# Moving a page compression by part of a unit against the delta-rule core that hides it

## The chip, the cores and the metric

The program runs on one core of one Trainium2 chip. The metric is the device time of one execution in microseconds: 1716.98 us is the median of three (1714.06 to 1723.23). TensorE (PE) multiplies, VectorE (DVE), ScalarE (ACT) and GpSimd (POOL) work on tiles, SyncE (SP) issues most transfers; a q behind an engine's name is its sequencer.

## What is computed

One inference step of a two-layer trunk: a gated DeltaNet layer and a sparse-attention layer (NSA), each followed by a gated feed-forward layer with a short convolution. There are 256 new tokens of one prompt and 8 x 8 tokens of running sequences, which have 1024 past positions in pages. Two parts matter here. The delta rule of 16 heads, evaluated in chunks:

```python
a_mat = where(stri, (kb @ k.T) * decay, 0) + eye          # unit lower triangular, inverted by levels
u, w = solve(a_mat, v * beta), solve(a_mat, kb * exp(gcum))
v_new = u - w @ s;  o = q_dec @ s + qk @ v_new;  s = s * g_tot + k_dec.T @ v_new
```

And the compression of the past pages, which needs nothing of the first layer and so is done beside it:

```python
first  = einsum('bnsgd,sdh->bngh', sub + pe[0], w1[0])    # sub: blocks of 16 past rows
second = einsum('bnsgd,sdh->bngh', sub + pe[1], w1[1])
hid = silu(first[:, :-1] + second[:, 1:]);  out = hid @ w2   # once for keys, once for values
```

## The kernel before, in words

The core stage works through eight **units** i = 0 to 7, in a loop of four run twice. A unit does the delta rule of one pair of heads (h = 0, 1) and the compression for two sequences: units 0 to 3 compress keys (v = 0), units 4 to 7 values (v = 1). No tile is doubled for the loop; each engine has one hand-written order, and semaphores counted by step name hold them together (`Steps.count(name, i)`).

*The delta rule on TensorE* (`pe_core_pair`, L1180): Gram products (L1191, L1198), turned keys (`ktok`, L1195), row broadcasts (L1206), then the inverse of the triangular matrix. Levels 1 to 4 are the **small products** (L1217, L1221: eight groups, `cp1`, `cx1` to `cp4`, `cx4`, 48 or 32 matmuls of 32 x 32), each waiting for VectorE (`dve_core`, L1394: masks, subtraction, transpose; the final spreading to full tiles X and Y is L1468). Levels 5 and 6 are full products (L1234, L1242, L1250), then come turned values (L1259), the state products (L1270, `ks`), v0, s1, ks1, v1, s2, o (L1277 to L1306) and the sample state update (L1316, `snew`).

*The compression* has 8 row groups m per unit. `turn_rows` (L1085): four transposes of raw page rows into the one bank 7. `copy_turned_rows` (L1136) on ScalarE: four copies out of the bank (L1143), which free it, and one rounding copy (L1146). `low_rows` (L1539, L1543) on POOL: the rest that rounding lost. `turned` has two buffers, by m % 2. `hidden_part` (L1097): 12 products for each m (L1107), cut in four **pieces** n = 4 m to 4 m + 3 of three products; the third product of piece 4 m + 2 is the first that reads the low part. `fill(lo, hi)` puts pieces lo to hi - 1 between the steps of the delta rule, where TensorE would wait. After piece 31 ScalarE applies silu (`hidden_silu`, L1151, with a table load), TensorE makes the **final product** (`compressed_rows`, L1118: L1125, L1132) into bank 7, and ScalarE stages it (`stage_compressed`, L1153).

The order of the turns before: turn 0 after the Gram products (L1200), 1 after the broadcasts, pieces 0 to 3, turn 2, pieces 4 to 7; pieces 8 to 15 between the small products, with turns 3 (at 9) and 4 (at 13); turn 5, 16, 17; level 5 with 18, 19, turn 6; level 6 with 20; 21 before `ks`; 22 and 23 after v0; s1, **turn 7** (L1286), ks1, 24 and 25, v1, 26 and 27, s2, o, 28 to 31, snew, final product.

*SP* (`sp_compress`, L1012) loads the raw rows in two halves x = 0, 1, one transfer of 64 KB for each of 16 pages, each with a page number read from SBUF (L1026). Half 0 holds the rows of turns 0 to 3, half 1 those of turns 4 to 7, and each is loaded for the next unit after turn 3 or 7 of this one. In order: half 0 of the next unit, half 1 of the next unit, then `store_pair` (L1028): after `snew` of each head the sample states (L1032) and the prompt state (L1033), then, after the staging copy, the compressed rows (L1036, L1038). Between units 3 and 4 it differs: half 0, eight loads of value weights (L1046, after each piece group of unit 3), `store_pair(3)`, and only then half 1.

*POOL* (`pool_core_pair`, L1537), in order: low parts 0 and 1, masks (`kmask`, L1552, after the key and query copies), a wait until the four state stores of the previous unit have landed (L1555), two state loads into the tiles so freed (L1557), low parts 2 to 6, two scalings of the state (L1562, after `ks`), low part 7, two spreads (L1567, after v0), for which snew waits. In unit 4 it also splits the value weights ahead of each low part (`split_w1`, L1529: L1533, L1535).

```python
            pool.wait_ge(state_out, STATES * i + 16)          # L1555
            for h in range(2):
                pool.dma_start(hd[h]["S0"], ...).then_inc(state_in, 16)
            for m in range(2, 7):
                low_rows(m)
```

Of the kernel before, what the change touches and what calls it, by code (L numbers as in the profile page):

```python
# [29 lines left out]
P = 128  # L30
# [198 lines left out]
def build(nc, ins, outs, where, base_cols):  # L229
    ctx = ExitStack()  # L230
    with ctx:
# [720 lines left out]
        for h in hd:  # L952
# [14 lines left out]
            pe=steps("core_pe", ["gram0", "ktok", "gram"] + both(["rows"])  # L967
# [7 lines left out]
            act=steps("core_act", both(["v"]) + ["ktok"] + both(["egc", "dec", "kdec", "r"]) + both(["qs"]) + both(["o"]) + ["k", "q"], lag=True),  # L975
            pool=steps("core_pool", ["lo0", "lo1", "kmask"] + [f"lo{m}" for m in range(2, 7)] + ["s0g0", "s0g1", "lo7", "spread0", "spread1"], lag=True))
# [31 lines left out]
            pe=steps("cmp_pe", ["t0", "t1", "u0"] + [x for m in range(2, 8) for x in (f"t{m}", f"u{m - 1}")] + ["h0", "u7", "o"], lag=True),  # L1008
            act=steps("cmp_act", [f"{x}{m}" for m in range(8) for x in "cr"] + ["h0", "h1", "s"], loop=True))
        H_BANK, T_BANK = (5, 6), 7  # L1010

        def sp_compress(sp):  # L1012
# [15 lines left out]
            def store_pair(g, v):  # L1028
# [5 lines left out]
                sp.wait_ge(C["act"].sem, C["act"].count("s", i))  # L1034
# [29 lines left out]
            sp.wait_ge(C["pe"].sem, C["pe"].count("o", UNITS_CMP - 1))  # L1064
# [20 lines left out]
        def turn_rows(pe, u, m):  # L1085
            if m % 4 == 0:
                pe.wait_ge(raw_in[m // 4], 256 * (u + 1))
            pe.wait_ge(C["act"].sem, C["act"].count(f"c{m - 1}", u) if m else C["act"].all_before(u))
# [3 lines left out]
            last.then_inc(C["pe"].sem, C["pe"].step(f"t{m}"))  # L1092
# [4 lines left out]
        def hidden_part(pe, u, v, n):  # L1097
            m, piece = n // 4, n % 4
            if piece == 0:
                pe.wait_ge(w1_split, 8 * v + m + 1)  # L1100
                pe.wait_ge(C["act"].sem, C["act"].count(f"r{m}", u))
            for t, half, part in HIGH_FIRST[3 * piece:3 * piece + 3]:
                if part == "low_rows" and t == 0 and half == 0:
                    pe.wait_ge(S5["pool"].sem, S5["pool"].count(f"lo{m}", u))
# [4 lines left out]
                if part == "low_rows" and half == 1:  # L1109
                    if t == 1:  # L1110
                        last.then_inc(C["pe"].sem, C["pe"].step(f"u{m}"))
# [6 lines left out]
        def compressed_rows(pe, u, v):  # L1118
            pe.wait_ge(C["act"].sem, C["act"].count("h1", u))
# [14 lines left out]
            last.then_inc(C["pe"].sem, C["pe"].step("o"))  # L1134

        def copy_turned_rows(act, u, m):  # L1136
            act.wait_ge(C["pe"].sem, C["pe"].count(f"t{m}", u))
            act.wait_ge(C["pe"].sem, C["pe"].count(f"u{m - 2}", u) if m >= 2 else C["pe"].count(f"u{m + 6}", u - 1))
# [5 lines left out]
            last.then_inc(C["act"].sem, C["act"].step(f"c{m}"))  # L1144
            act.wait_ge(C["act"].sem, C["act"].count(f"c{m}", u))
            act.copy(turned_high[m % TURNED], turned[m % TURNED]).then_inc(C["act"].sem, C["act"].step(f"r{m}"))  # L1146

        def hidden_silu(act, u, v, t):
            act.wait_ge(C["pe"].sem, C["pe"].count("h0" if t == 0 else "u7", u))
            act.wait_ge(C["pe"].sem, C["pe"].count("o", u - 1))  # L1150
            act.activation(cmp_hid[t].rearrange("p (x n) -> p x n", x=8), psum[:, H_BANK[t], 0:4 * NC2].rearrange("p (n x) -> p x n", x=8), ACT.Silu, bias=pe_bias[:, 2 * v + t:2 * v + t + 1]).then_inc(C["act"].sem, C["act"].step(f"h{t}"))  # L1151

        def stage_compressed(act, g, u, v):  # L1153
            act.wait_ge(C["pe"].sem, C["pe"].count("o", u))
# [7 lines left out]
            ins_.then_inc(C["act"].sem, C["act"].step("s"))  # L1162
# [7 lines left out]
        def pe_core(pe):  # L1170
            pe.sem_inc(S5["pe"].sem, S5["pe"].first)
            pe.sem_inc(C["pe"].sem, C["pe"].first)
# [3 lines left out]
            for v in range(2):  # L1176
                with pe.Fori(0, 4) as g:
                    pe_core_pair(pe, g + 4 * v, v)

        def pe_core_pair(pe, i, v):  # L1180
# [3 lines left out]
            def fill(lo, hi):  # L1184
                for n in range(lo, hi):
                    hidden_part(pe, i, v, n)
# [5 lines left out]
            last.then_inc(pe_steps.sem, pe_steps.step("gram0"))  # L1192
            pe.wait_ge(dve_steps.sem, dve_steps.all_before(i))
            for u in range(3):
                last = pe.transpose(psum[:, B_BANK[1], u * P:(u + 1) * P], kS[:, u * P:(u + 1) * P], ident)  # L1195
            last.then_inc(pe_steps.sem, pe_steps.step("ktok"))
            for rhs, cols in ((kS, G_COLS), (qS, Q_COLS)):
                last = pe.matmul(psum[:, A_BANK[0], cols], kS[:, TP:TP + P], rhs[:, TP:T], start=True, stop=True)  # L1198
            last.then_inc(pe_steps.sem, pe_steps.step("gram"))
            turn_rows(pe, i, 0)  # L1200
            pe.wait_ge(dve_steps.sem, dve_steps.all_before(i))
            for q, banks in ((0, A_BANK), (1, B_BANK)):
                for h in range(2):
                    if q == 1 and h == 1:
                        pe.wait_ge(act_steps.sem, act_steps.count("ktok", i))
                    last = pe.matmul(psum[:, banks[h], 0:T], row_ones[h], row_src[h][:, q, :], start=True, stop=True)  # L1206
                    if q == 1:
                        last.then_inc(pe_steps.sem, pe_steps.step(f"rows{h}"))
# [1765 lines left out]
```

## Time and profile before

| | |
|---|---|
| three executions | 1716.98, 1714.06, 1723.23 us |
| span of the profiled execution | 1715.5 us |
| mean granted clock of TensorE | 0.943 of full |
| busy: PE, DVE, ACT, POOL | 90%, 56%, 47%, 17% |
| core stage, first Gram product to last final product | 254.8 to 712.1 us |
| units 0 to 7 | 57.1, 55.0, 54.9, 54.7, 62.8, 55.4, 55.3, 62.1 us |

The profiled execution is one more execution: its span runs from the first to the last instruction, and lies 1.5 us under the median of the executions, which also have what lies around the instructions. Times in rows are from the span's start; a number in brackets is the idle time of the engine ahead of the group, with what ended it.

### The profile page before, as it was taken

The numbers are of one execution on the slowest core, as the hardware profiler recorded it, in microseconds if no ns is written. First come the engines' busy times: TensorE is split into PE (matmuls) and PEld (weight loads), VectorE is DVE, ScalarE is ACT, GpSimd is POOL, SyncE is SP. The second block draws the span as 40 slices with busy tenths as digits, with TensorE's granted clock in tenths as the row PEclk, the third lists the DMA queues.
The fourth block names the chain that finished last, engine by engine and source line by source line (L and its number), as shares of the span: only waits on it lengthen the run. The fifth ranks groups of instructions, "written<-read, shape, count | busy, mean of one in ns | idle before, by whom it ended". The sixth has DMA issues, their size and how long they took to land.

```text
span 1715.5 us, 38118 instructions
## 1 busy us (share of the span) xinstructions
PE 1539.0 (90%) x13678; PEld 1348.7 (79%) x13678; DVE 952.5 (56%) x1749; ACT 800.6 (47%) x1579; POOL 300.1 (17%) x492
## 2 busy tenths in 40 slices
PE   6999979999988998899999999966777778999897
PEld 6999847777757776579999999954555558999897
DVE  5775245554655454464777644434655556777732
ACT  5675325665555555443444533224444535444521
POOL 1331033433454332200000001031112100000000
PEclk9999969999999998979999999997898987999999
DMA  7444232322432232425555658444534414555650
GB/s 179 147 144 157 102 117 58 95 76 59 125 100 71 66 89 75 112 66 147 148 147 147 174 134 227 128 151 143 169 98 161 132 50 123 147 147 147 164 135 31
DMA packets 285294, 209.56 MB, mean 122 GB/s; under 512 B 29231, under 2 KB 277071, under 8 KB 284768
## 3 DMA queue, kind: packets, MB, share of 16 engines
q1 hardware_dynamic: 275926, 176.32, 36.9%
q0 software_dynamic: 9248, 31.80, 6.0%
q8 instruction: 45, 0.74, 0.2%
q10 hardware_dynamic: 42, 0.44, 0.1%
q14 instruction: 33, 0.27, 0.1%
HBM read 185.67 MB, written 22.85 MB: 122 GB/s over the span
## 4 chain that ended last, share of the span: by engine, by line
PE 74%; DVE 8%; ACT 7%; issue 5%; DMA 2%; SPq 1%; POOL 1%; POOLq 1%; DVEq 0%; ACTq 0%
PE psum L621 15%; PE psum L622 15%; PE psum L623 15%; PE psum L1107 7%; ACT sbuf_resident L2429 2%; PE psum L1221 1%; PE psum L2226 1%; PE psum L1091 1%; PE psum L2381 1%; DMA sbuf_resident<-in_nsa_w_in_dram 1%; PE psum L1610 1%; PE psum L915 1%; PE psum L1270 1%; PE psum L1234 1%; PE psum L1250 1%
## 5 line engine op out<-in xcount | busy, mean ns | idle before, releaser
L621 PE MATMUL psum<-h_rounded,weights_low 128*128 128x320 f32 x1248 | 392.0, 314 | 1.9 <-DVE weights_low L597 1.9
L623 PE MATMUL psum<-h_rounded,weights_high 128*128 128x320 f32 x1248 | 387.0, 310 | 0.0
L622 PE MATMUL psum<-weighted_x_low,weights_high 128*128 128x320 f32 x864 | 267.2, 309 | 0.0
L621 PEld LDWEIGHTS psum<-h_rounded,weights_low 128*128 128x128 f32 x1248 | 235.2, 188 | 5.1 <-DVE weights_low L597 2.1
L597 DVE TENSOR_TENSOR weights_low<-sbuf_resident,weights_high 128x2048 fp32r<-128x2048 f32 x90 | 205.7, 2288 | 55.1 <-ACT weights_high L582 55.1
L623 PEld LDWEIGHTS psum<-h_rounded,weights_high 128*128 128x128 f32 x1248 | 235.1, 188 | 0.0
L582 ACT CAST weights_high<-sbuf_resident 128x2048 fp32r<-128x2048 f32 x90 | 170.1, 1893 | 95.1 <-PE psum L623 64.8
L622 PEld LDWEIGHTS psum<-weighted_x_low,weights_high 128*128 128x128 f32 x864 | 165.9, 192 | 0.2
L1143 ACT COPY sbuf_resident<-psum 64x256 f32<-64x256 f32 x256 | 108.5, 424 | 91.3 <-PE psum L1091 88.8
L696 DVE SCALAR_TENSOR_TENSOR sbuf_stages<-sbuf_stages,sbuf_resident 128x344 f32<-128x344 f32 (+1 forms) x184 | 105.6, 574 | 55.5 <-ACT sbuf_stages L678 51.7
L1543 POOL TENSOR_TENSOR turned_low<-sbuf_resident,turned_high 128x512 fp32r<-128x512 f32 x64 | 76.8, 1200 | 265.3 <-ACT turned_high L1146 265.2
L678 ACT ACTIVATE sbuf_stages<-sbuf_stages,sbuf_resident 128x336 f32<-128x336 f32 (+1 forms) x76 | 44.1, 581 | 165.0 <-DVE sbuf_stages L1774 164.0
L622 PE MATMUL psum<-weights_low,weights_high 128*128 128x320 f32 x384 | 118.8, 309 | 0.0
L686 POOL COPY sbuf_stages<-sbuf_stages 128x2 f32<-128x2 f32 (+1 forms) x76 | 30.8, 405 | 494.5 <-DVE sbuf_stages L1774 417.8
L621 PE MATMUL psum<-hidden_high,weights_low 128*128 128x320 f32 x352 | 110.9, 315 | 6.3 <-ACT sbuf_resident L1731 5.4
L1107 PE MATMUL psum<-turned_high,w_low 128*128 128x504 f32 x256 | 114.6, 448 | 1.9 <-POOL w_low L1535 1.9
L622 PE MATMUL psum<-hidden_low,weights_high_wide 128*128 128x320 f32 x352 | 110.0, 313 | 0.0
L623 PE MATMUL psum<-hidden_high,weights_high_wide 128*128 128x320 f32 x352 | 109.8, 312 | 0.0
L1107 PE MATMUL psum<-turned_high,w_high 128*128 128x504 f32 x256 | 106.6, 416 | 0.0
L1107 PE MATMUL psum<-turned_low,w_high 128*128 128x504 f32 x256 | 75.1, 400 | 2.8 <-POOL turned_low L1543 2.8
L1645 DVE TENSOR_TENSOR sbuf_resident<-sbuf_resident,psum 128x320 f32<-128x320 f32 x24 | 11.7, 487 | 118.1 <-PE psum L623 118.1
L622 PEld LDWEIGHTS psum<-weights_low,weights_high 128*128 128x128 f32 x384 | 73.4, 191 | 0.0
(438 smaller groups left out, 3147.7 us busy)
## 6 DMA issues: line engine op xcount, KB each, us to landing
sbuf_resident<-in_ffn_w_up_dram SPq DMA_DIRECT2D x88, 512.0 KB, 4.9
sbuf_resident<-in_gdn_w_in_dram SPq DMA_DIRECT2D x48, 512.0 KB, 4.7
sbuf_resident<-in_ffn_w_down_dram SPq DMA_DIRECT2D x32, 704.0 KB, 6.3
sbuf_resident<-in_cache_nsa_kv_dram SPq DMA_DIRECT2D x256, 64.0 KB
sbuf_stages<-in_state_gdn_s_dram POOLq DMA_DIRECT2D x16, 512.0 KB, 5.3
out_gdn_s_sample_dram<-sbuf_stages SPq DMA_DIRECT2D x16, 512.0 KB, 3.8
sbuf_resident<-in_gdn_w_out_dram SPq DMA_DIRECT2D x16, 512.0 KB, 5.5
sbuf_stages<-in_cache_nsa_kv_dram POOLq DMA_DIRECT2D x64, 128.0 KB, 3.4
```

The lines of the kernel that those rows point to most:

```text
L582: act.copy(dst[:, 0:kn * P], slot(w)[:, 0:kn * P]).then_inc(hi_done, 1)
L597: eng.tensor_tensor(ring_lo[w % RING][:, 0:kn * P], sl, hi[:, 0:kn * P], ALU.subtract).then_inc(lo_done, 1)
L621: pe.matmul(out, w_lo, x_hi_tile, start=first, stop=False)
L622: pe.matmul(out, w_hi, x_lo_tile, start=False, stop=False)
L623: return pe.matmul(out, w_hi, x_hi_tile, start=False, stop=last)
L678: return act.activation(y[:, 0:n_out], xp[:, 0:n_out], ACT.Copy, scale=tap)
L686: pool.tensor_copy(tail[:, 0:hist], xp[:, TP:TP + hist])
L696: dve.scalar_tensor_tensor(out=y[:, 0:n_out], in0=xp[:, n:n + n_out], scalar=taps(n), in1=y[:, 0:n_out], op0=ALU.mult, op1=ALU.add).then_i ...
L1107: last = pe.matmul(psum[:, H_BANK[t], 0:4 * NC2], weights[:, 8 * half + m, t * P:(t + 1) * P], rows, start=(m == 0 and half == 0 and part ...
L1143: last = act.copy(dst, src)
L1543: pool.tensor_tensor(turned_low[m % TURNED], turned[m % TURNED], turned_high[m % TURNED], ALU.subtract).then_inc(pool_steps.sem, pool_step ...
L2429: return act.activation(s, s, ACT.Exp, bias=mx_p[:, h, x:x + 1], accum_out=sm_p[:, h, x:x + 1])
```

## The change

Each unit's turn 0 and its copy, rounding and low part move to the end of the previous unit; for unit 0 they stand ahead of the loop. The final product and the staging copy move into the next unit, behind pieces 1 to 3 and behind the exponentials `egc`; those of unit 7 stand behind the loop. The first and last unit and unit 4 have bodies of their own, with the counts adjusted. SP's order and the order of its waits stay; its wait for the staging copy is for the moved copy. POOL's order stays but for low part 0, now the last of the previous unit. The core of the diff, as the new order of TensorE:

```diff
+            turn_rows(pe, i, 1)                # after the first Gram products
+            fill(0, 1)
             pe.wait_ge(dve_steps.sem, dve_steps.all_before(i))
-            ktok transposes; late Gram products; turn_rows(pe, i, 0); row broadcasts (h = 1 waits for ktok's copy)
-            turn_rows(pe, i, 1)
-            fill(0, 4)
-            turn_rows(pe, i, 2)
-            fill(4, 8)
+            late Gram products; row broadcasts
+            fill(1, 4)
+            if place != "first":
+                compressed_rows(pe, i - 1, before)
+            pe.wait_ge(dve_steps.sem, dve_steps.count("bts1", i))
+            ktok transposes
+            turn_rows(pe, i, 2, first=place == "first")      # waits for the staging copy of i - 1
+            fill(4, 10)
+            turn_rows(pe, i, 3)
+            fill(10, 12)
+            pe.wait_ge(act_steps.sem, act_steps.count("ktok", i))
             for k in range(1, SMALL):
...
-                    n = 8 + 2 * (k - 1) + (name == "cx")
-                    if n % 4 == 1:
-                        turn_rows(pe, i, 3 + (n - 8) // 4)
+                    n = 12 + 2 * (k - 1) + (name == "cx")
                     fill(n, n + 1)
-            turn_rows(pe, i, 5)
-            fill(16, 18)
+                    if n in (13, 17):
+                        turn_rows(pe, i, 4 if n == 13 else 5)
+            fill(20, 21)
...
-                fill(18 if k == SMALL else 20, 19 if k == SMALL else 21)
+                fill(21 if k == SMALL else 23, 22 if k == SMALL else 24)
...
-                    fill(19, 20)
                     turn_rows(pe, i, 6)
+                    fill(22, 23)
...
-                    fill(21, 22)               # ahead of ks
+                    fill(24, 25)
...
-            fill(22, 24)                       # behind v0; turn 7 stays behind s1
+            fill(25, 27)
...
-            fill(24, 26)                       # behind ks1
+            fill(27, 28)
...
-            fill(26, 28)                       # behind v1
+            if place != "last":
+                turn_rows(pe, i + 1, 0)
+            fill(28, 30)
...
-            fill(28, 32)                       # behind o
+            fill(30, 32)
...
-            compressed_rows(pe, i, v)
```

(Lines such as "late Gram products; row broadcasts" put several statements in words.) Two waits are new: piece 0 waits for the previous unit's second silu, and turn 2 for its staging copy. ScalarE's new order:

```diff
-            v copies; ktok; copy_turned_rows 0; egc; dec; copy_turned_rows 1, 2; kdec; 3, 4, 5; r; qs; 6, 7; o; k, q; silu; stage
+            copy_turned_rows 1; egc; stage of i - 1; dec; ktok; 2; v copies; 3; kdec; 4, 5, 6; r; qs; 7; 0 of i + 1; o; k, q; silu
```

And POOL's:

```diff
+            if split:
+                split_w1(pool, v, 0)
-            low_rows(0)
-            low_rows(1)
+            low_part_of(1)
             kmask; wait for the state stores; state loads; low parts 2 to 6; s0g; low part 7; spreads
+            if not is_last:
+                low_rows(pool, i + 1, 0).then_inc(pool_steps.sem, pool_steps.step("lo0next"))
```

## Rows read from the trace of the kernel before

**Rows 1.** The profile page: busy time by engine, and the chain that ended last.
```profile
PE 1539.0 (90%) x13678; PEld 1348.7 (79%) x13678; DVE 952.5 (56%) x1749; ACT 800.6 (47%) x1579; POOL 300.1 (17%) x492
...
PE 74%; DVE 8%; ACT 7%; issue 5%; DMA 2%; SPq 1%; POOL 1%; POOLq 1%; DVEq 0%; ACTq 0%
```

**Rows 2.** Stretches, units 2 and 4: length; busy PE, PEld, DVE, ACT, POOL; clock, DMA.
```profile
366.90:421.80 54.90, 51.94 (x664) 40.51 (x662) 30.95 (x76) 31.07 (x70) 18.96 (x16) 1.00 0.29 82
...
476.50:539.30 62.80, 54.69 (x680) 42.46 (x678) 31.18 (x76) 31.31 (x70) 32.12 (x30) 0.95 0.30 82
```

**Rows 3.** Timeline of TensorE, unit 2; the last two lines are of units 4, 7.
```profile
371.88 0.66 PE L1091 MATMUL psum<-sbuf_resident 128*128 128x128 f32 x4 [0.82 <-ACT sbuf_resident L1143]
...
376.79 0.66 PE L1091 MATMUL psum<-sbuf_resident 128*128 128x128 f32 x4 [1.28 <-ACT sbuf_resident L1143]
...
478.78 1.34 PE L1206 MATMUL psum<-sbuf_stages,sbuf_resident 16*128 16x320 f32 x8
...
660.44 0.66 PE L1091 MATMUL psum<-sbuf_resident 128*128 128x128 f32 x4 [2.56 <-ACT sbuf_resident L1143]
```

**Rows 4.** Timelines of TensorE, SP and POOL, from turn 7 of unit 1.
```profile
354.49 0.60 PE L1091 MATMUL psum<-sbuf_resident 128*128 128x128 f32 x4
...
378.24 0.62 SPq L1033 DMA_DIRECT2D out_gdn_s_prompt_dram<-sbuf_stages  x1
...
382.30 1.80 POOL L1557 DMA_DIRECT2D sbuf_stages<-in_state_gdn_s_dram  x2 [2.02 <-DMA out_gdn_s_prompt_dram<-sbuf_stages]
384.11 1.29 POOL L1543 TENSOR_TENSOR turned_low<-sbuf_resident,turned_high 128x512 fp32r<-128x512 f32 x1
...
385.78 0.39 PE L1107 MATMUL psum<-turned_low,w_high 128*128 128x504 f32 x1
...
409.32 0.60 PE L1091 MATMUL psum<-sbuf_resident 128*128 128x128 f32 x4
...
410.10 20.20 SPq L1026 DMA_DIRECT2D sbuf_resident<-in_cache_nsa_kv_dram  x16
```

**Rows 5.** Timelines of TensorE and VectorE in unit 2: small products and spreading.
```profile
380.96 0.23 PE L1217 MATMUL psum<-sbuf_resident 128*32 128x8 f32 x2 [0.53 <-DVE sbuf_resident L1439]
...
381.67 0.50 PE L1107 MATMUL psum<-turned_high,w_low 128*128 128x504 f32 x1
...
382.55 0.23 PE L1217 MATMUL psum<-sbuf_resident 128*32 128x8 f32 x2
...
392.41 0.23 PE L1217 MATMUL psum<-sbuf_resident 128*32 128x8 f32 x2
...
393.83 1.92 DVE L1468 TENSOR_TENSOR sbuf_stages<-sbuf_resident 128x256 f32<-128x256 f32 x4
...
395.53 1.05 PE L1234 MATMUL psum<-sbuf_stages 128*128 128x128 f32 x8
```

**Rows 6.** Timelines of ScalarE, POOL and TensorE in unit 2, behind turn 7.
```profile
410.03 1.74 ACT L1143 COPY sbuf_resident<-psum 64x256 f32<-64x256 f32 x4 [1.21 <-PE psum L1091]
...
414.93 2.28 POOL L1567 TENSOR_TENSOR sbuf_stages<-sbuf_stages,sbuf_resident 64x512 f32<-64x512 f32 x2
...
421.75 1.16 PE L1191 MATMUL psum<-sbuf_stages 128*128 128x128 f32 x8
```

**Rows 7.** Unit 7: timelines of POOL and TensorE; a stretch (columns as rows 2).
```profile
671.12 0.89 POOL L1557 DMA_DIRECT2D sbuf_stages<-in_state_gdn_s_dram  x1 [4.41 <-issue]
...
673.35 0.49 PE L1107 MATMUL psum<-turned_low,w_high 128*128 128x504 f32 x1 [2.81 <-POOL turned_low L1543]
...
673.35:685.81 12.46, 12.46 (x216) 8.98 (x217) 4.47 (x14) 3.39 (x8) 2.27 (x2) 0.73 0.10 35
```

**Rows 8.** Timelines of SP and TensorE in unit 4.
```profile
478.78 1.19 SPq L1036 DMA_DIRECT2D compressed_keys<-sbuf_resident  x1
481.51 23.43 SPq L1026 DMA_DIRECT2D sbuf_resident<-in_cache_nsa_kv_dram  x18
...
504.55 1.11 PE L1091 MATMUL psum<-sbuf_resident 128*128 128x128 f32 x4 [2.20 <-DMA sbuf_resident<-in_cache_nsa_kv_dram]
```

More of the change, by code:

```diff
@@ L966, in build @@
         S5 = dict(
-            pe=steps("core_pe", ["gram0", "ktok", "gram"] + both(["rows"])
+            pe=steps("core_pe", ["gram0", "gram"] + both(["rows"]) + ["ktok"]
                      + [f"{x}{k}" for k in range(1, SMALL) for x in ("cp", "cx")]
@@ L1007, in build, with c_count, low_rows_count @@
         C = dict(
-            pe=steps("cmp_pe", ["t0", "t1", "u0"] + [x for m in range(2, 8) for x in (f"t{m}", f"u{m - 1}")] + ["h0", "u7", "o"], lag=True),
-            act=steps("cmp_act", [f"{x}{m}" for m in range(8) for x in "cr"] + ["h0", "h1", "s"], loop=True))
+            pe=steps("cmp_pe", ["t1", "u0", "o_prev", "t2", "u1"] + [x for m in range(3, 8) for x in (f"t{m}", f"u{m - 1}")] + ["t0next", "h0", "u7"], lag=True),
+            act=steps("cmp_act", ["c1", "r1", "s_prev"] + [f"{x}{m}" for m in range(2, 8) for x in "cr"] + ["c0next", "r0next", "h0", "h1"], lag=True))
+        def c_count(eng, name, u):
+            if name in ("t0", "c0", "r0"):
+                if isinstance(u, int) and u == 0:
+                    return C[eng].first - (name == "c0")
+                return C[eng].count(f"{name}next", u - 1)
+            if name in ("o", "s"):
+                if isinstance(u, int) and u == UNITS_CMP - 1:
+                    return C[eng].all_before(UNITS_CMP, 1)
+                return C[eng].count(f"{name}_prev", u + 1)
+            return C[eng].count(name, u)
+        def low_rows_count(m, u):
+            return S5["pool"].count("lo0next", u - 1) if m == 0 else S5["pool"].count(f"lo{m}", u)
         H_BANK, T_BANK = (5, 6), 7
@@ L1171, in pe_core @@
             pe.sem_inc(S5["pe"].sem, S5["pe"].first)
[L1172 removed]
+            pe.sem_inc(C["pe"].sem, C["pe"].first - 1)
             pe.wait_ge(pads, 11)
@@ L1175, in pe_core, with pe_core_pair @@
             pe.wait_ge(bias_act, 2)
[L1176 to L1180, printed above, removed]
+            turn_rows(pe, 0, 0, first=True)
+            pe_core_pair(pe, 0, 0, "first")
+            with pe.Fori(1, 4) as i:
+                pe_core_pair(pe, i, 0)
+            pe_core_pair(pe, 4, 1)
+            with pe.Fori(5, 7) as i:
+                pe_core_pair(pe, i, 1)
+            pe_core_pair(pe, 7, 1, "last")
+            compressed_rows(pe, 7, 1, last_unit=True)
+        def pe_core_pair(pe, i, v, place=None):
+            before = 0 if place != "first" and (v == 0 or isinstance(i, int) and i == 4) else 1
             pe_steps, dve_steps, act_steps, pool_steps = S5["pe"], S5["dve"], S5["act"], S5["pool"]
@@ L1332, in act_core @@
                 take(act, 0, x).then_inc(S5["act"].sem, 1)
-            for v in range(2):
-                with act.Fori(0, 4) as g:
-                    act_core_pair(act, g, g + 4 * v, v)
+            copy_turned_rows(act, 0, 0, first=True)
+            act_core_pair(act, 0, 0, 0, "first")
+            with act.Fori(1, 4) as i:
+                act_core_pair(act, i, i, 0)
+            act_core_pair(act, 4, 4, 1)
+            with act.Fori(5, 7) as i:
+                act_core_pair(act, i - 4, i, 1)
+            act_core_pair(act, 3, 7, 1, "last")
+            stage_compressed(act, 3, 7, 1, last_unit=True)
         def take(act, i, x):
@@ L1365, in act_core_pair @@
                 last.then_inc(act_steps.sem, act_steps.step(f"kdec{h}"))
-            for m in range(3, 6):
+            for m in range(4, 7):
                 copy_turned_rows(act, i, m)
```

151 lines of the change are left out of this document (84 added, 67 removed).

## The prediction

> **What bounds the kernel now.** I read the page first: TensorE is busy 90% of the span and carries 74% of the chain that ended last [rows 1]. The change lies wholly in the core stage, 254.8 to 712.1 us, eight units of 54.7 to 62.8 us. The table of stretches gives one line per unit [rows 2]: TensorE's own work is about 52 us of a regular unit, so at most some 3 us a unit is idle. The TensorE timeline of unit 2 shows where: 0.82 us before the second turn and 1.28 us before the third (ScalarE's copy holds the one bank), and 0.53 us before the first small product (VectorE; [rows 5]). In the value units, where a table load stands ahead, the third turn waits 2.56 us [rows 3]. This is what the change can win.
>
> Next I looked for a second limit behind the first, and there is one, a loop through four queues [rows 4]. Turn 7 of unit 1 starts at 354.49 and frees the second raw buffer. SP then issues 16 page loads (in the next unit the same 16 take 20.20 us, 1.26 us each), and only behind them the four state stores, the last at 378.24. POOL waits for its landing, issues the next state loads at 382.30 (1.80 us), and only behind these makes the low part of row group 2 (384.11 to 385.40). TensorE's first low-row product of piece 10 runs at 385.78. So the **lag** from turn 7 to the low part being ready is 385.40 - 354.49 = 30.9 us, and TensorE comes 0.4 us after it. Then it takes 409.32 - 385.78 = 23.5 us to turn 7 of this unit. The loop 30.9 + 23.5 = 54.4 us is nearly as long as the unit, 54.83. It is full already, and nothing in the diff changes SP's order or POOL's order around the wait for the stores.
>
> **The change part by part**
>
> Gains, if nothing else bound. Turn 0 moves to the end of the previous unit, so turn 1 follows the first Gram products; the waits of [rows 3] go, and so does the broadcasts' wait for the copy of the turned keys. The final product of the compression moves behind pieces 1 to 3. I lay out TensorE from the unit's start: Gram 1.0 us, turn 1 0.5, piece 0 0.7, late Gram 0.4, broadcasts 1.34 (as where nothing holds them, [rows 3]), pieces 1 to 3 2.05 (a piece is three products 0.227 us apart, 0.68), final product 1.0, key transposes 0.35, turn 2 with a short wait for the staging copy 0.7, pieces 4 to 9 4.1 and about 0.3 of waiting for group 2, turn 3 0.5, two products of piece 10 0.55. Its first low-row product is wanted at **13.6 us**.
>
> From there to turn 7. Between that product and the level-5 products the new order has pieces 10 to 20, the old one 10 to 17; it also has three more small products. Spacings of [rows 5]: 0.71 us for a small product of 48 blocks (0.55 with 32), 0.88 for a piece between two, 0.45 for a turn. In order: rest of pieces 10 and 11 0.96; small, 12, small, 13, turn 4, to 4.5; small, 14, small, 15, to 7.7; the four small ones of levels 3 and 4 with 16, 17, turn 5 and 18 between, the last starting at 12.45. In the old order pieces 15 to 17 and a turn followed it; now only 19 and 20 (1.9 us with the product) cover VectorE's spreading of X and Y, whose third piece ends 395.3, 2.9 us after the last small product's start (392.41). So the level-5 products start at 15.35 us (0.95 of it a new wait) instead of 395.53 - 385.78 = 9.75. From them to turn 7 both orders have six pieces: 13.79 us. Sum **29.1 us** instead of 23.5.
>
> From turn 7 to the unit's end 12.43 us were used [rows 6]. Three pieces fewer (2.0) and the final product gone (1.0), turn 0 added (0.4), and pieces 28 and 29 now wait 0.7 us for ScalarE's copy of turn 7 (410.03 to 412.4): about **10.1 us**. The POOL spreads still end 7.9 us after turn 7 and just make it. Unhindered, a unit would be 13.6 + 29.1 + 10.1 = 52.9 us, 1.9 less than now.
>
> The loop. The lag stays 30.9, for its loads, stores and POOL steps are the same. But the low part of group 2 is now wanted 10.1 + 13.6 = 23.7 us after turn 7, not 31.3: TensorE stands **7.2 us** at piece 10 in units 1, 2, 3, 5, 6 and 7. Everything else behind POOL's wait (low parts 3 to 6) is later in the order and covered. The period becomes 31.0 + 29.1 = 60.1 us, plus the clock.
>
> The clock. Unit 7 has this very stall: POOL's second state load is held back 4.41 us to 671.12, group 2 is late, TensorE waits 2.81 us, and the same work that took 9.75 us in unit 2 (385.78 to 395.53) takes 12.46 at a mean granted clock of 0.73 [rows 7], so 6.7 us of it at half clock (1.2 GHz): 2.7 us lost. Unit 4 has two stalls over 2 us and a mean clock of 0.95 over 62.8 us [rows 2]: 3.1 us lost, 1.5 each. I take 2.0 per stall, between the two, with bounds 0 (no fall) and 4 (half clock well into the large pieces). The Trainium skill, TensorE: Matmul & The Clock Gate, section "HAM oscillation", says that a loop with a wait in every turn re-enters each turn at half clock and pays 1.67 us of throttled time, half of it lost; by that estimate each stall would cost 0.8 and the sum below would be 8 us less. The trace's own 1.5 and 2.7 decide.
>
> Unit 4, the first of the values. Here SP stores unit 3's states and its compressed keys before it loads the second raw half. The staged keys are now ready some 7.5 us into unit 4, not at 0.6. In the trace the first of these loads starts 481.51 - 478.78 = 2.7 us after the keys' store and the last lands 23.0 us later, 28 us into the unit, and turn 4 waited 2.20 us for it [rows 8]. Now it lands at 7.6 + 2.7 + 23.0 = 33.3 us, and turn 4, moved before the second pair of small products, wants it at 17.7: a stall of **15.6 us**, one time. POOL's splits of the value weights, which cost about 2 us there, are hidden by it. From turn 4 to turn 7 25.1 us, plus 2.0 clock.
>
> Parts with one answer: the table load, the v copies, the earlier ktok and decay exponentials lie in ScalarE's idle time (31 of 55 us busy) [rows 2]; peeled loop bodies add program, not work. Unit 0 loses its waits and the closing product, 2.9 us; its state loads wait for nothing. The stage's tail (staging copy, store, closing) is the same; the last unit ends about 11.5 us after turn 7, not 12.55.
>
> **The sum**, as starts of turn 7. Unit 0 starts at 254.8, lasts 57.1 - 2.9 and 0.3 for its first turned copy, and its turn 7 is 10.1 before its end: 299.2. Units 1, 2, 3 each 31.0 + 29.1 + 2.0 = 62.1 later: 485.5. Unit 4 starts 10.1 later at 495.6; 33.3 + 25.1 + 2.0 gives 556.0. Units 5 and 6, 62.1 each: 680.2. Unit 7: the late second load repeats (I take it as bound to the count of loads), 62.1 + 4.4: 746.7. End at 758.2 instead of 712.1: **+46.1 us**. Nothing after the stage moves. The profiled execution spans 1715.5 us against a median of 1716.98 (1.5 outside the span or run to run); I add to the median: **1763 us**. Bounds: clock 0 instead of 2, seven times, -14; the late load not repeated, -4; clock 4, +14.
>
> **The rivals**
>
> A. The stalls come but the clock stays full: 1749, and 1745 if the late load doesn't return either. Against it: units 4 and 7, both at half clock after less idle [rows 2, 7].
>
> B. The clock stays half through most of the 29 us after each stall: about 1777. For it: that stretch begins with small products, which left unit 7 at half clock for 6.7 us; against it: it did return.
>
> C. Faster. Piece 10 doesn't wait, because stores or loads come sooner than in the trace; only the raw wait of unit 4 stays. It decides at a lag of 23.7 us: the 16 loads would have to take 13.0 us, 0.8 each. Then: unit 0 -2.9, units 1 to 3 together -5.9, unit 4 +7.7, units 5 and 6 -4.9, unit 7 -7.8, so -13.8 and 1703 us. For it: only that the 2.6 us of waits a unit are real [rows 3, 5]. Against: the 1.26 us repeats in every unit, and the loads carry an address read each. [...]
>
> D. Loads half as much faster: gain and loss cancel, about 1717.
>
> **How the numbers follow.** Forecast 0.62 (1763 with 2 us of clock), A 0.17, B 0.11, C 0.06, D 0.04. A measurement of this kernel can tell about 0.5% (8.6 us) from no change. Slower by more: forecast, A, B, 0.90; within 0.04; faster 0.06. The range reaches from A's 1742 (both its parts and a little of unit 4) to B's 1779; C and D and a little beyond stay out.
>
> **What would show it.** A TensorE idle of about 7 us before a low-row product, ended by POOL, in six units, each followed by half clock; POOL waiting about 10 us for the state store instead of 2 (its mask work is done 7 us into the unit, the store lands at 17.7); one idle near 15 us in unit 4, ended by a page load; regular units near 62 us; the waits for ScalarE's turned copies gone. The forecast is wrong if units are 53 us and POOL's low part 2 ends before TensorE asks, or if the lag differs from 31 us.

## The result and the profile after

The changed kernel takes **1785.87 us** (median of four, 1780.51 to 1790.01), the kernel before in the same series 1720.11 (1714.06 to 1725.36): a ratio of 1.0366, 95% interval 1.0327 to 1.0405, so some 66 us slower. The forecast was 1763 with a range of 1742 to 1779. The direction and the mechanism held; the size didn't.

The page of the changed kernel, busy time and chain, beside [rows 1]:

```profile
PE 1565.7 (88%) x13678; PEld 1362.4 (76%) x13678; DVE 938.7 (53%) x1749; ACT 797.5 (45%) x1578; POOL 296.3 (17%) x492
...
PE 74%; DVE 6%; ACT 5%; issue 5%; SPq 4%; DMA 3%; POOL 1%; POOLq 1%; DVEq 0%; ACTq 0%
```

The span of this execution is 1787.3 us. The same 13678 matmuls run, but SP's queue has gone from 1% to 4% of the chain and DMA from 2% to 3%. The stretches of units 2 and 4, columns as in [rows 2]:

```profile
372.75:436.59 63.84, 55.46 (x664) 42.51 (x662) 28.07 (x76) 30.80 (x72) 18.33 (x16) 0.92 0.25 70
499.62:573.50 73.88, 56.74 (x663) 43.70 (x662) 33.64 (x76) 30.97 (x72) 31.92 (x30) 0.84 0.24 69
```

Unit 2 is 8.9 us longer, and only 3.5 of that is busy time of TensorE (the same products at a lower clock); the rest is idle. The units from 0 on last 54.2, 64.0, 63.8, 63.0, 73.9, 64.6, 63.0 and 70.8 us (54.7 to 62.8 before). The stage ends at 771.8 instead of 712.1: **59.7 us** later.

TensorE's waits in the stage (the line in front is who waits, then what released it: us in total, times, longest):

```profile
PE psum L1131 <- POOL turned_low L1592: 45.9, 6, 11.0
PE psum L1113 <- DMA sbuf_resident<-in_cache_nsa_kv_dram: 12.6, 1, 12.6
PE psum L1274 <- DVE sbuf_stages L1519: 11.5, 8, 2.7
...
PE psum L1113 <- ACT sbuf_resident L1174: 2.3, 7, 0.3
```

The last line is what the change was able to win: the waits of [rows 3], 17.0 us over 14 times before, are 2.3. The first is what it paid. How one of the six comes about, in the timelines of TensorE, SP and POOL from turn 7 of unit 1 on, beside [rows 4]:

```profile
362.54 0.60 PE L1113 MATMUL psum<-sbuf_resident 128*128 128x128 f32 x4
...
363.33 20.05 SPq L1041 DMA_DIRECT2D sbuf_resident<-in_cache_nsa_kv_dram  x16
...
385.98 0.62 SPq L1048 DMA_DIRECT2D out_gdn_s_prompt_dram<-sbuf_stages  x1
...
389.93 1.80 POOL L1613 DMA_DIRECT2D sbuf_stages<-in_state_gdn_s_dram  x2 [10.54 <-DMA out_gdn_s_prompt_dram<-sbuf_stages]
391.75 2.32 POOL L1592 TENSOR_TENSOR turned_low<-sbuf_resident,turned_high 128x512 fp32r<-128x512 f32 x2
...
393.08 2.05 PE L1131 MATMUL psum<-turned_low,w_high 128*128 128x504 f32 x4 [6.72 <-POOL turned_low L1592]
```

Read it downwards: turn 7 frees the raw buffer; SP spends 20.05 us on 16 loads; the fourth state store stands behind them; POOL waits 10.54 us for its landing, and behind that wait stands the low part that TensorE wants. From 362.54 to 393.08 it is 30.5 us, forecast 31.0.

### The profile page after: what moved, and what is told of

Read it like the earlier page. It is cut to its first block, busy times and chain, and to the rows that moved or that the text cites. A ratio compares the mean times of both kernels' runs of the same rounds, so it can differ in the third digit from the quotient of the medians.

```text
span 1787.3 us, 37786 instructions
## 1 busy us (share of the span) xinstructions
PE 1565.7 (88%) x13678; PEld 1362.4 (76%) x13678; DVE 938.7 (53%) x1749; ACT 797.5 (45%) x1578; POOL 296.3 (17%) x492
## 4 chain that ended last, share of the span: by engine, by line
PE 74%; DVE 6%; ACT 5%; issue 5%; SPq 4%; DMA 3%; POOL 1%; POOLq 1%; DVEq 0%; ACTq 0%
PE psum L621 14%; PE psum L623 14%; PE psum L622 14%; PE psum L1131 8%; SPq L1036 2%; PE psum L1262 2%; PE psum L2284 1%; PE psum L1113 1%; ACT sbuf_resident L2487 1%; DMA out_gdn_s_prompt_dram<-sbuf_stages 1%; SPq L1041 1%; PE psum L2439 1%; DMA sbuf_resident<-in_nsa_w_in_dram 1%; PE psum L1274 1%; PE psum L1668 1%
## 5 line engine op out<-in xcount | busy, mean ns | idle before, releaser
L1131 PE MATMUL psum<-turned_low,w_high 128*128 128x504 f32 x256 | 82.8, 427 | 45.9 <-POOL turned_low L1592 45.9
L1131 PEld LDWEIGHTS psum<-turned_low,w_high 128*128 128x128 f32 x256 | 48.7, 203 | 56.8 <-POOL turned_low L1592 48.4
```

What stands on the lines that cost most here:

```text
L1131: last = pe.matmul(psum[:, H_BANK[t], 0:4 * NC2], weights[:, 8 * half + m, t * P:(t + 1) * P], rows, start=(m == 0 and half == 0 and part ...
```

## Experiments

**1. The loop, opened at POOL: in both orders.** The edit, the same in the changed kernel and (for the second run) in the kernel before:

```diff
+            for m in range(2, 4):
+                low_part_of(m)
             pool.wait_ge(state_out, STATES * i + 16)
             ...                                     # the two state loads
-            for m in range(2, 7):
+            for m in range(4, 7):
                 low_part_of(m)
```

> After, with POOL's wait for the previous unit's state stores and the two state loads moved behind the low parts of groups 2 and 3. Nothing else changes. Theory (the low part queued behind that wait holds TensorE 45.9 us in six units, and each stall drops the clock): the six waits for POOL go, regular units take 53 to 54 us instead of 63 to 64.5, only unit 4 keeps its wait of about 13 us for page loads; about 1706 us (1700 to 1715), the state loads still land before ks. Rival (the new order of the pieces is what costs, POOL only shows up as the last of several semaphores): the wait changes its name, units stay over 60 us, over 1770. Rival (the moved state loads are late for ks instead): units near 58.

> Before, with the same move in POOL's order. Theory: in the old order TensorE comes 0.4 us after the low part, so regular units stay at 54.8 and 55.4 us; only unit 7's wait of 2.81 us for POOL and its half clock (2.7 us) go: 3 to 6 us less, about 1715. Rival (the loop already costs in every unit of before): more than 1 us less per unit, under 1710.

In the changed kernel: 1727.59 us, ratio to before 1.002 (0.9987 to 1.0053). TensorE's waits:

```profile
PE psum L1113 <- DMA sbuf_resident<-in_cache_nsa_kv_dram: 13.7, 1, 13.7
PE psum L1274 <- DVE sbuf_stages L1519: 10.9, 8, 2.7
PE psum L1131 <- ACT turned_high L1177: 4.7, 9, 1.0
```

All six waits for POOL are gone, and with them 58 us: one queue position, with no work added or taken away. Regular units last 54.06 to 54.66 us at full clock. But the kernel is not faster than before, and the 1700 to 1715 us expected are missed: unit 4 takes 75.4 us, since its page loads are as late as they were, and the gain in a regular unit is 0.8 us, not 1.9. In the kernel before the edit shows no gain where 3 to 6 us were expected: 1720.05, ratio 1.0011 (0.9985 to 1.0037). Unit 7's wait of [rows 7] went, but unit 4's wait for its pages [rows 8] grew from 2.20 to 6.55 us. Only 1.6 us of that growth is TensorE coming earlier; the pages themselves are ready 2.8 us later in the unit, though SP starts loading them at the same time (481.41 and 481.51). What moved is POOL's two state loads, from 490.35 to 498.44, in among the last pages (first line of the kernel before, the other two of this run):

```profile
490.35 1.80 POOL L1557 DMA_DIRECT2D sbuf_stages<-in_state_gdn_s_dram  x2
```

```profile
498.44 1.80 POOL L1559 DMA_DIRECT2D sbuf_stages<-in_state_gdn_s_dram  x2
...
507.24 1.11 PE L1091 MATMUL psum<-sbuf_resident 128*128 128x128 f32 x4 [6.55 <-DMA sbuf_resident<-in_cache_nsa_kv_dram]
```

That these loads hold up the pages fits the times; it was not tried by itself.

**2. The two halves of the change.** Only turn 0, the final product and the staging copy stay moved; pieces and turns 3 to 7 are put back among the steps of the delta rule where they were:

```diff
-            fill(4, 10)
-            turn_rows(pe, i, 3)
-            fill(10, 12)
+            fill(4, 8)
...
-                    n = 12 + 2 * (k - 1) + (name == "cx")
+                    n = 8 + 2 * (k - 1) + (name == "cx")
```

> After, with the pieces and turns 3 to 7 put back where they were before; only turn 0, the final product and the staging copy stay skewed. Theory: the low-row product of piece 10 is wanted behind cp1, cx1 and cp2 again, and TensorE now waits for x0 ahead of cp1 (about 3 us); it stands some 2 us for POOL in each of six units instead of 7. The loop is 31 + 23.5 = 54.5 us plus the clock, so units of 55 to 57 us; unit 4 waits less for the raw half, about 8 us. About 1728 us (1718 to 1740). Rival (the skew itself costs, not where the pieces went): near after, 1775 or more.

1730.62 us, ratio 1.0038 (1.0005 to 1.0071). Of the 66 us some 55 come from the **respreading** of the pieces, which moved the first want of piece 10's low row from 19 us into the unit (in this run as in [rows 4]) to 13.4 to 14.1 (units of experiment 1). The skew alone waits for POOL 7.8 us in all, 4.4 of it in unit 7, and 1.5 us a unit for VectorE ahead of the first small product.

**3. The clock behind a stall.** 26 products that nothing uses are put ahead of piece 10 in the six units that stall, so that TensorE works through most of the wait:

```diff
             turn_rows(pe, i, 3)
+            for x in range(26): pe.matmul(...)     # 128x504, into a bank that is overwritten
             fill(10, 12)
```

> After, with 26 extra products of 504 columns (5.9 us) ahead of piece 10 in units 1, 2, 3, 5, 6, 7, into a bank that is free there; their result is overwritten and used by nothing. They fill most of the 7 us for which TensorE stands. Theory (of the 18.2 to 19.9 us from the low-row product to level 5, 15.3 would be the work and 3 to 4.5 the clock that falls in the stall): the clock stays full, that stretch takes 15.5 to 16 us, the units take 60 to 61 us, 18 to 22 us less in all, about 1765. Rival (the stretch is longer for another reason, VectorE's chain or program fetching): no change, or up to 6 us more where the filler delays piece 10.

1768.02 us, ratio 1.0298 (1.0253 to 1.0342): **faster for 26 products more** in each of six units, by 18 us in the medians. The two ratios come from different series and their intervals just overlap; in the two traces the stage ends 12.9 us earlier. TensorE in unit 2 of this run, and then the same steps of the changed kernel without the filler:

```profile
383.81 6.08 PE L1254 MATMUL psum<-turned_high,w_high 128*128 128x504 f32 x26
...
391.46 1.17 PE L1131 MATMUL psum<-turned_low,w_high 128*128 128x504 f32 x4 [1.13 <-POOL turned_low L1595]
...
393.27 0.50 PE L1131 MATMUL psum<-turned_high,w_low 128*128 128x504 f32 x1
...
404.11 0.23 PE L1261 MATMUL psum<-sbuf_resident 128*32 128x8 f32 x2
...
407.56 1.18 PE L1277 MATMUL psum<-sbuf_stages 128*128 128x128 f32 x8 [1.28 <-DVE sbuf_stages L1522]
```

```profile
396.06 0.79 PE L1131 MATMUL psum<-turned_high,w_low 128*128 128x504 f32 x1
...
401.24 0.71 PE L1262 MATMUL psum<-sbuf_resident 32*32 32x32 f32 x48
401.88 0.50 PE L1131 MATMUL psum<-turned_high,w_low 128*128 128x504 f32 x1
...
412.52 0.71 PE L1274 MATMUL psum<-sbuf_stages 128*128 128x128 f32 x4 [1.27 <-DVE sbuf_stages L1519]
```

The first product of piece 12 takes 0.50 us with the filler and 0.79 without. From the low row to level 5 it is 407.56 - 391.46 = 16.1 us, at a mean clock of 1.00, against 412.52 - 393.08 = 19.4. Units 1, 3 and 6 take 16.1 too, but units 5 and 7 take 17.4 and 17.6 at 0.90 and 0.89: there the clock fell in spite of the filler (in unit 7, 5.5 us of waiting were still left behind it). TensorE is at half clock (1.2 GHz) from the stall to about 401.5, over 8 us (granted clock 0.50 from 393.08 to 401.24), and then back at 2.4. So the clock's share of a stall is measured by itself: 3.3 us in this unit.

**4. Unit 4's pages.** With POOL's order kept as in experiment 1, SP issues the second raw half for unit 4 ahead of unit 3's stores:

```diff
-                    for m in range(8):
+                    for m in range(6):
+                        load_w1_values(m)
+                    next_raw(0, 1, 1, 3)
+                    for m in range(6, 8):
                         load_w1_values(m)
                 store_pair(3, v)
-                if v == 0:
-                    next_raw(0, 1, 1, 3)
```

> The changed kernel with both queues mended: POOL waits for the state stores only behind low parts 2 and 3, and SP issues the second raw half for unit 4 ahead of the last two loads of value weights and of unit 3's stores. My theory: in unit 4 only the raw load holds TensorE (12.6 us in the changed kernel, 13.7 with POOL's order alone); without it the unit falls from 75.4 to 56 to 59 us (POOL's splits of the weights may then show with some 2 us), the other units stay at 54.1 to 54.7, and the kernel takes 1706 to 1712 us, 0.5 to 0.9% less than the kernel before. Rival 1: the unit's length is set by its extra POOL work and by the exponentials and copies of the first value unit; then the wait changes its releaser, the unit stays over 65 us and the time over 1718. Rival 2: half of unit 4's excess is half clock behind the stall; that would return too and belongs to the first theory's lower end.

**1704.07 us**, ratio 0.9895 (0.9851 to 0.9938): faster than both kernels. Unit 4 falls from 75.4 to 60.1 us with no wait for DMA left; the first theory held, a little above its 56 to 59. The same edit to SP without POOL's:

> The changed kernel with SP's order mended alone. Theory: unit 4 falls from 73.9 us to what the POOL loop allows, 62 to 64 us if the loop of the state stores binds there as in its neighbours (unit 4's POOL wait was not seen because SP's raw wait came last), so 10 to 12 us less than the changed kernel, about 1775. Rival: nothing else holds unit 4, because unit 3 ends with no raw loads between turn 7 and the state stores; then unit 4 takes 55 to 58, 16 to 19 us less, about 1768, or the raw loads now issued ahead of the stores put the same loop there for the first time and unit 4 gains a POOL wait of some 7 us.

1779.91 us, ratio 1.0299 (1.0244 to 1.0355). Unit 4 is 68.0 us, above what either expected, and its wait has a new releaser; the rival's last clause came closest, with 11.3 us instead of 7:

```profile
519.25 1.80 POOL L1614 DMA_DIRECT2D sbuf_stages<-in_state_gdn_s_dram  x2 [11.96 <-DMA out_gdn_s_prompt_dram<-sbuf_stages]
...
523.07 0.79 PE L1132 MATMUL psum<-turned_high,w_low 128*128 128x504 f32 x1 [11.32 <-POOL w_low L1589]
```

With the pages ahead of the stores, unit 4 gets the loop that the other units have, and with more on POOL: the split of a weight stands ahead of the low part. Unit 4 had been spared the loop only because its pages came after the stores. The two mends are worth 58 us (POOL) and 6 us (SP) alone, by the medians, and 82 together; by the ratios, each to the kernel before in its own series, SP's is worth 11.

This run also has the six stalls of the changed kernel once more, 6.6 to 7.6 us and 10.5 in unit 7, with the same work behind them. From the low row to level 5 it takes 17.5 to 20.0 us, so 1.4 to 3.9 more than at full clock and **2.3 on average**. The dearest and the one behind the longest stall (columns as in [rows 2]):

```profile
393.42:413.41 19.99, 18.73 (x376) 13.26 (x376) 7.54 (x24) 4.62 (x10) 3.36 (x3) 0.76 0.33 86
...
720.04:737.67 17.63, 16.43 (x375) 11.66 (x375) 7.46 (x24) 4.62 (x10) 3.35 (x3) 0.89 0.09 29
```

**5. Is the respreading worth anything with both queues mended?** The skew alone, and the kernel before, each with both mends:

> Turn 0, final product and staging moved as in the change, pieces and turns 3 to 7 where they were before, and both queues mended. Theory: with the queues out of the way the place of the pieces costs little; this order has VectorE's wait ahead of the turned... of the first Gram-side product (1.52 us a unit) where the changed one waits for the spreading (1.26): units of 54.4 to 54.8, unit 4 at 58 to 60, about 1714 us, within 0.3% of the fully changed kernel with both queues mended. Rival: the respreading is worth what it was meant for once POOL is out of the way; then this one is over 5 us slower than that one.

> The kernel before with both queues mended. Theory: unit 4's load wait (6.6 us with POOL's order alone, 2.2 before) goes and the unit falls to 57 to 60 us; unit 7's late state load stays harmless; others stay at 55.0 to 55.5: 3 to 7 us less than before, about 1714. Rival: unit 4 is bound by POOL's splits and the table load and stays over 62: no difference (1720).

1713.11 us (ratio 0.9898, 0.9853 to 0.9943) and 1719.44 (0.9962, 0.9932 to 0.9992; its unit 4 takes 58.2 us, as the theory had it). The ratio of the skew alone is that of the full change, though the medians (1713.11 and 1704.07) are 9 us apart. The traces are finer: its regular units take 54.7 to 56.4 us (2.5 us of waiting for VectorE in each) against 54.0 to 54.6, and its stage ends 5.4 us later (below). For the whole time that rival is neither shown nor excluded.

**6. The loop, opened at SP.** POOL's order as in the changed kernel; of the 16 loads of the second half eight go ahead of the state stores and eight behind them. That mends unit 4's pages too (its first eight go ahead of the last two value weights):

```diff
-                    for x in range(2):
-                        next_raw(g + 1, v, x, g + 4 * v)
-                    store_pair(g, v)
+                    next_raw(g + 1, v, 0, g + 4 * v)
+                    next_raw(g + 1, v, 1, g + 4 * v, early)
+                    store_pair(g, v, lambda: load_raw(g + 1, v, 1, pages=late))
```

> The changed kernel with POOL's order as it is and only SP's changed: of the 16 loads of the second raw half eight are issued behind turn 7, then the four state stores, then the other eight (in unit 3 the first eight stand ahead of the last two value weights). If the loop is what the trace says, the lag from turn 7 to POOL's low part 2 falls from 31 us: 1 + 8 x 1.26 = 11.1, the stores then wait for the last state update (some 12 to 13 us behind turn 7) and are landed by 18, two state loads and the low part make 21 to 22 us, under the 23.8 at which TensorE asks. All six waits for POOL vanish, regular units 54.1 to 54.7 us, and the last eight loads land some 27 us behind turn 7, just ahead of turn 4 (28.4): about 1705 to 1710, as with POOL's order and the raw half mended. Rival 1: the late loads miss turn 4 by 1 to 4 us in every unit, then half clock follows it: units of 57 to 60, about 1735. Rival 2: it is the landing of the stores, not their place behind the loads, that takes the time; the waits stay near 7 us and the time near 1775.

1715.51 us, ratio 0.9927 (0.9894 to 0.9961). SP and POOL behind turn 7 of unit 1, which starts at 352.49:

```profile
353.27 9.55 SPq L1041 DMA_DIRECT2D sbuf_resident<-in_cache_nsa_kv_dram  x8
...
365.78 0.62 SPq L1048 DMA_DIRECT2D out_gdn_s_prompt_dram<-sbuf_stages  x1
367.98 9.68 SPq L1041 DMA_DIRECT2D sbuf_resident<-in_cache_nsa_kv_dram  x8
...
369.70 1.80 POOL L1617 DMA_DIRECT2D sbuf_stages<-in_state_gdn_s_dram  x2 [0.37 <-issue]
...
373.82 1.40 POOL L1596 TENSOR_TENSOR turned_low<-sbuf_resident,turned_high 128x512 fp32r<-128x512 f32 x1 [2.31 <-ACT turned_high L1181]
```

POOL no longer waits for the store, and low part 2 ends 22.7 us behind turn 7, held by its own input; the two state loads are issued after 19.0. Five of six waits for POOL are gone with nothing changed on POOL. So it was the place of the stores behind the loads. Regular units last 54.05 to 54.7 us, but for unit 3, where the late half of the loads is just too late for turn 4 (54.9 us):

```profile
435.67 0.65 PE L1117 MATMUL psum<-sbuf_resident 128*128 128x128 f32 x4 [0.65 <-DMA sbuf_resident<-in_cache_nsa_kv_dram]
```

Unit 7 still waits for its low part, 2.98 us, and the stretch from there to level 5 takes 19.9 us at a mean clock of 0.75, where experiment 4 has 16.5 at 1.00. That is most of the 6.0 us by which the stage ends behind experiment 4's, and part of why this comes out above 1705 to 1710; the rest of the kernel, further down, is the other part.

**7. Cover for VectorE's spreading.** Experiment 4's kernel, with one piece more ahead of level 5:

```diff
-            fill(20, 21)
+            fill(20, 22)
...
-                fill(21 if k == SMALL else 23, 22 if k == SMALL else 24)
+                fill(22 if k == SMALL else 23, 23 if k == SMALL else 24)
...
                     turn_rows(pe, i, 6)
-                    fill(22, 23)
```

> The kernel with both queues mended (1704 us), and piece 21 moved ahead of level 5, 22 ahead of its second product, none behind turn 6: 0.68 us more of TensorE's work stands in the 1.26 us in which it waits for VectorE's spreading. Theory: the wait falls to about 0.6 in each unit and nothing new is late behind turn 6: regular units 53.4 us instead of 54.07, 5 us less in all, about 1699 beside 1704. Rival: the spot behind turn 6 is as tight, TensorE then waits there for VectorE or ScalarE by as much, units stay at 54.1.

**1697.71 us**, ratio 0.9854 (0.9794 to 0.9914), the lowest median. With four executions the interval overlaps that of experiment 4; that it is the faster of the two is shown by the stage, which ends 8.2 us earlier, not 5. Units 1 to 3 last 53.4 us, as expected; units 5 and 6 54.0 (54.6 before this edit). Unit 4 gains most of what was not expected, 60.1 to 56.4.

## Why the prediction was right and wrong

**Right, and shown by the runs.** The loop of [rows 4]: moving its POOL end (1) takes all six waits away, moving its SP end (6) five of six. The forecast's waits for POOL are six of 7.2 us and 4.4 for the late load, 47.6; measured 45.9. The lag to the first low row, summed over the six units, was to be 6 x 31.0 + 4.4 = 190.4 us and is 190.5. Unit 7's second state load was late again:

```profile
718.63 0.93 POOL L1613 DMA_DIRECT2D sbuf_stages<-in_state_gdn_s_dram  x1 [11.09 <-DMA out_gdn_s_prompt_dram<-sbuf_stages]
723.94 0.89 POOL L1613 DMA_DIRECT2D sbuf_stages<-in_state_gdn_s_dram  x1 [4.38 <-issue]
```

And unit 4's pages: forecast 33.3 us into the unit, measured 32.75, in TensorE's timeline:

```profile
532.37 1.12 PE L1113 MATMUL psum<-sbuf_resident 128*128 128x128 f32 x4 [12.60 <-DMA sbuf_resident<-in_cache_nsa_kv_dram]
```

The wait is 3 us under the 15.6 forecast because TensorE itself came 20.15 us into the unit, not 17.7.

**Wrong: the end of the stage, 758.2 forecast, 771.8 measured.** The 13.6 us, term by term:

- *"I take 2.0 per stall"*: the six stretches from low row to level 5 last 18.7, 19.4, 18.2, 19.4, 18.2 and 19.9 us, against 16.1 at full clock (experiment 3). That is 17.4 us in all, **2.9 per stall** (2.1 to 3.8) where I had 12.0: +5.4 us. I chose the middle of 1.5 and 2.7 and gave the stall of 2.81 us in [rows 7] no more weight than unit 4's; the nearer row was that one, with the same kind of products behind the stall. Part of it is chance, though: the same stalls lost 2.3 each in the trace of SP's mend alone (experiment 4), and the price doesn't follow the length, for a stall of 10.5 us lost 1.5 there and one of 2.98 us lost 3.8 in experiment 6. The value was inside my bounds of 0 to 4, but I took it on the low side. A cheap and the dearest stretch (columns as in [rows 2]):

```profile
457.34:475.57 18.23, 16.95 (x375) 11.94 (x376) 7.54 (x24) 4.61 (x10) 3.35 (x3) 0.85 0.41 99
...
726.17:746.11 19.94, 18.73 (x376) 13.29 (x376) 7.47 (x24) 4.64 (x10) 3.36 (x3) 0.75 0.08 26
```

- *"So the level-5 products start at 15.35 us"*: 16.1 where nothing is slow, six times +0.75, so **+4.5 us**. From the last small product to level 5 it takes 407.56 - 404.11 = 3.45 us, where I had read 2.9 off a unit of the old order; the small products before it take the other 0.2. VectorE starts its spreading 1.42 us behind the last small product in both orders, but the same four instructions take 1.92 us in the old one [rows 5] and 2.44 in the new. The traces show what goes with it: a low part of POOL that runs at the same time for 0.38 us in the old order and 0.89 in the new. In unit 7 of the kernel before, with nothing on POOL beside them, they take 1.70. Unit 2 of the kernel before, the same step with the filler, and unit 4 of the changed kernel, where low part and weight split overlap them by 2.95 us and they take 3.85:

```profile
392.92 1.29 POOL L1543 TENSOR_TENSOR turned_low<-sbuf_resident,turned_high 128x512 fp32r<-128x512 f32 x1 [5.34 <-ACT turned_high L1146]
```

```profile
405.33 1.09 POOL L1595 TENSOR_TENSOR turned_low<-sbuf_resident,turned_high 128x512 fp32r<-128x512 f32 x1 [5.23 <-ACT turned_high L1177]
...
405.53 2.44 DVE L1522 TENSOR_TENSOR sbuf_stages<-sbuf_resident 128x256 f32<-128x256 f32 x4
```

```profile
544.17 1.09 POOL L1592 TENSOR_TENSOR turned_low<-sbuf_resident,turned_high 128x512 fp32r<-128x512 f32 x1 [5.00 <-ACT turned_high L1177]
544.44 3.85 DVE L1519 TENSOR_TENSOR sbuf_stages<-sbuf_resident 128x256 f32<-128x256 f32 x4
...
545.20 0.81 POOL L1586 CAST w_high<-sbuf_resident 128x512 fp32r<-128x512 f32 x1
546.09 1.32 POOL L1588 TENSOR_TENSOR w_low<-sbuf_resident,w_high 128x512 fp32r<-128x512 f32 x1
```

  No edit moved POOL's work away from the spreading, so the cause is read off the traces and not tried. The same error, with a wait of 0.5 us for ScalarE's rounding copy that the stalls hide, makes the unhindered unit 54.07 instead of 52.9 (the other three parts of it agree to 0.2 us), which is why the regular units gained so little in experiment 1.
- *Unit 4, "25.1 us, plus 2.0 clock"*, with POOL's splits *"hidden by it"*: from turn 4 to turn 7 it took 30.9, +3.8. In regular units of experiment 4 that part takes 25.75. But the page stall is not the whole of what makes it long: unit 4 of experiment 4 has no page wait and takes 31.5 us there. Both traces have the slow spreading above, which TensorE waits for 2.68 us instead of 1.26, and a second fall of the clock behind it (0.66 over the next 5.1 us here, 0.52 over 6.3 us in experiment 4). So by these traces POOL's splits were not hidden. With the pages 0.55 early and 0.1 behind turn 7 the term is +3.4.
- Unit 0 -0.7, level 5 to turn 7 +0.3, lags +0.1, the tail +0.4.

Together +13.4 of 13.6. The gap to rival B (1777, half clock through most of the 29 us) is closed in time but not in kind: the clock does return, some 8 us behind the stall. The estimate of 0.8 us per stall, worked out from the 1.67 us of the Trainium skill, TensorE: Matmul & The Clock Gate, section "HAM oscillation", is too low here: against experiment 3 the changed kernel lost 2.9.

**Wrong or not, but missed: "nothing after the stage moves".** Between the two profiled executions it does, by another 12 us. The stretch from the first product behind the stage's tail to the span's end, with the mean clock before the DMA share; first of the kernel before, then of the changed one, then of experiments 5 (the kernel before with both mends) and 4 (the change with both mends):

```profile
719.18:1715.50 996.32, 883.78 (x6833) 807.17 (x6833) 562.69 (x947) 417.25 (x766) 77.94 (x230) 0.93 0.49 137
```

```profile
778.79:1787.30 1008.51, 897.33 (x6833) 814.62 (x6833) 562.52 (x947) 417.52 (x766) 77.90 (x230) 0.91 0.48 135
```

```profile
711.04:1719.80 1008.76, 897.95 (x6833) 814.82 (x6833) 562.56 (x947) 417.71 (x766) 77.91 (x230) 0.91 0.49 135
```

```profile
704.10:1698.80 994.70, 880.33 (x6833) 803.68 (x6833) 562.11 (x947) 417.28 (x766) 77.91 (x230) 0.93 0.49 137
```

The same 6833 products take either about 996 us at 0.92 to 0.93 or about 1009 at 0.90 to 0.91, and both lengths come with either order of the units: in twelve profiled executions six of each (994 to 999, and 1006 to 1012). So it seems to belong to the execution: the ten of experiment 1's changed kernel fall in two groups as well, 1715.9 to 1720.7 us and 1727.5 to 1733.8. Whether the change shifts how often each comes, these runs don't tell. It is why an edit is best read by where the stage ends. By that same product (719.2 before, 778.8 after) experiment 1 has 720.6, 4 704.1, 5 709.5 and 711.0, 6 710.1 and 7 695.9: 23 us ahead of before. The forecast's 22.9 us of error are then 13.6 of the stage, 3.1 by which the kernel before itself came out higher than in the first three runs, and 6 that are left over. They can lie in this rest, but no trace measures them.

**Rival C** (faster if the lag were under 23.7 us) can now be judged too. Its condition was right about the waits: at a lag of 22.7 us (experiment 6) units 1 to 3, 5 and 6 no longer wait for POOL. Its price was not. Experiment 1 is nearest to it, with no wait for POOL and unit 4's pages late as in C, and its stage ends 1.4 us later than before where C had it 13.8 earlier: regular units gain 0.8 us instead of 2 to 2.5, and unit 4 loses 12.6 instead of 7.7. Experiment 6 gains its 0.7% with unit 4's pages mended as well (59.5 us).

## What to carry to other kernels

When work is moved earlier against a loop that runs over several queues, add up the loop's lag (from what frees a buffer, through every instruction ahead of the one that matters on each queue, to the consumer) and compare it with the new distance between the two; the old slack of 0.4 us said that no piece reading a low row could come earlier. Mend the queue orders first and together: in the kernel before, POOL's alone changed nothing, since the wait for the pages grew in its place, and the skewed order pays only where both the low part and unit 4's pages come in time (experiments 4 to 7). A forecast stall should be priced with the clock behind it, and as a range: stalls of the same work lost 1.4 to 3.9 us here. And when an order changes, look at which engines now work at the same time: a step read off the old order (2.9 us) can be longer in the new one (3.45).

## What was unexpected of the hardware

- A stall of 6.5 to 7.7 us costs TensorE 2.1 to 3.3 us more at half clock afterwards in one trace and 1.4 to 3.9 in another, with no clear relation to its length; 26 useless products during it brought that back whole in four units of six.
- VectorE's four spreading instructions take 1.70 us with nothing on POOL beside them, 1.9 to 2.0 with 0.4 us of POOL's work beside them, 2.4 with 0.9 and 3.85 with 2.95.
- Unit 7's second state load is held up by 4.41 us in the kernel before, 4.38 in the changed one and 4.1 to 4.4 in all experiments but the sixth, whose 6.39 us are these:

```profile
648.14 0.92 POOL L1617 DMA_DIRECT2D sbuf_stages<-in_state_gdn_s_dram  x1 [1.03 <-DMA out_gdn_s_prompt_dram<-sbuf_stages]
655.45 0.89 POOL L1617 DMA_DIRECT2D sbuf_stages<-in_state_gdn_s_dram  x1 [6.39 <-issue]
```

  It is the last of the 16 loads in each trace; what holds it was not tried.
- The rest of the kernel has two lengths, 12 us apart, with the clock.
